# Writing out the feed-forward loops of a two-layer decoder kernel, and giving each modulation slab its own tabled place

## The chip, the cores and the metric

One core of one Trainium2 chip runs the whole program: TensorE (PE), VectorE (DVE), ScalarE (ACT), GpSimd (POOL) and SyncE (SP), each with its own instruction stream, tied together by semaphores. The metric is device time of one execution in microseconds; lower is better. Before the change it was 2439.5 us (median of 3 runs, 2437.03 to 2441.91).

## The reference

Two layers of a decoder, 256 tokens, width D = 2048, all in float32:

```python
for l in range(2):
    mod = silu(c) @ w_mod[l] + b_mod[l]                 # 12288 values
    sh1, sc1, g1, sh2, sc2, g2 = split(mod, 6)
    u = x * (1 + sc1) + sh1
    proj = u @ w_in[l]                                  # 2048 x 6144: q k v B C h
    attn = dilated_mixture(rotary(q), rotary(k), v)     # 8 heads
    conv = B * conv3(C * h)
    mixed = group_rms_norm([attn, conv]) * gain
    x = layer_norm(alpha * x + (1 + g1) * (mixed @ w_out[l]))
    u = x * (1 + sc2) + sh2
    ff = relu(u @ w_ff1[l]) ** 2 @ w_ff2[l]             # hidden width 8192
    x = layer_norm(alpha * x + (1 + g2) * ff)
```

## The kernel before

**Units and groups.** The large products are cut into units. A unit is 512 output columns over a contraction of 2048, for both 128-token tiles. It has eight groups (j = 0 to 7) of 256 contraction rows, and a group is 12 matmuls of 128x128 by 128x512: each float32 weight is split into a high and a low part, each activation too, and hi·hi, lo·hi and hi·lo are summed (L1150 to L1152). A layer is a mixer of 16 units (12 of `w_in`, 4 of `w_out`) and a feed-forward part of 32 units: four blocks of 4 units up (`w_ff1`) and 4 down (`w_ff2`). Below, a place "p" in a part is 8 · unit + j, and a side job at p comes behind group p.

**The path of a weight.** SP loads a group's weights (512 KB) into one of four `raw` buffers as soon as `lo_ready` says that DVE has read it. ACT copies it to `w_hi` (L388) once PE has finished the group four back; DVE subtracts and writes `w_lo` (L677); PE multiplies.

**Modulation.** `w_mod` is 24 slabs of 1024 columns by 2048 rows, each 16 chunks of 512 KB. POOL loads chunks into four `mod_raw` buffers as they come free. DVE multiplies each chunk by the condition and adds it to one of two accumulators `mod_acc` (L688 for the first of a slab, L692 for the rest). When a slab's 16 chunks are in, it has to be summed over the partitions by PE before its accumulator is used again: `reduce_slab` does it with 8 matmuls with one column (L1175), and DVE adds the bias into `mod_col`. A gate is wanted along the free axis, on all partitions: `gate_slab` (L1195) does that with two 128x512 matmuls, and DVE adds the result to `gate`, into which the bias has been loaded by a broadcast DMA. Slabs 0 to 3 are made in the start, 4 to 9 in the first mixer, 10 to 17 in the first feed-forward part and 18 to 23 in the second mixer; the second feed-forward part has no chunks. Each layer has 12 slabs; its first gate is slabs 4 and 5 (16 and 17 in the second layer), its last gate slabs 10 and 11 (22 and 23).

**What sets the order.** Each engine's order is written by hand. In the mixers it is written out, with side jobs at tabled places (`MIX_MOD_AT` for chunks, `RED_AT` for sums). In the feed-forward part PE, ACT and DVE run a loop of three turns over 8 units (`Fori`, L1380, L624, L1036), and the last 7 units are written out behind it. In the first layer's loop there are four chunks per unit, and PE sums a slab behind (v, j) = (4, 1) and (7, 7), where the second one's last chunk is at (7, 6). The last gate of the first layer is summed into `mod_col` like the others, and then brought to the free axis by `gate_rows`: 16 matmuls (L1186) and four copies on ACT. The gates of slabs 16, 17 and 22, 23 are left in `mod_acc` until the next fill unit.

**Fill units.** Between two parts x is normalised: DVE's residual and statistics, ACT's normalisation, PE's transposes (L1203), ACT's and DVE's split. The unit that follows is a fill unit (fills 1, 2 and 3 stand between the four parts). In fills 2 and 3 PE sums both gate slabs behind j = 5. In fill 1 the sum of slab 9 comes first: PE does it at the mixer's end and DVE reads it within `statistics`.

**Hidden activations.** After an up unit ACT makes relu and square into `hid`, PE transposes it (behind j = 2 of the next unit), and ACT and DVE split it into `m_hi` and `m_lo`. All transposes and sums share two PSUM banks `tb` in a fixed numbering of jobs.

Of the kernel before, what the change touches and what calls it, by code (L numbers as in the profile page):

```python
# [30 lines left out]
ALU = mybir.AluOpType  # L31
# [38 lines left out]
LOOP_H = (0, 2, 4, 6)  # L70
MOD_LAYER = MIX_SLABS + 8
# [16 lines left out]
def taken(layer):  # L88

    return set(Q_AT[layer] + K_AT[layer] + O_AT[layer] + Z_AT + B_AT + R_AT  # L90
               + [start + 3 for g in range(2) for start in HEAD_AT[layer][g]])
# [3 lines left out]
RED_AT = [[min(p for p in range(MIX_MOD_AT[layer][KC * (i + 1) - 1] + 2, 8 * U_MIX) if p not in taken(layer))  # L95
           for i in range(MIX_SLABS - 1)] for layer in range(DEPTH)]


def gate_half(layer, i):

    first = 0 if layer == 0 else 4
    return i - first if i - first in (0, 1) else None
# [13 lines left out]
def transpose_jobs():  # L116
# [8 lines left out]
    for layer in range(DEPTH):  # L125
        modded = layer < DEPTH - 1
        if layer == 0:
            for q in range(START_SLABS):
                add(("start turn", 2 * q), 1)
                add(("start", q), 1)  # L130
                add(("start turn", 2 * q + 1), 1)
        else:
            add(("fill", 2 * layer), 8)
            add(("rows", 2 * layer), 4)
        side = []
        for g in range(2):
# [5 lines left out]
        side += [(p, -1, 0, "red", 2 if layer == 0 and i < 2 else 1, i) for i, p in enumerate(RED_AT[layer])  # L142
                 if not (layer and gate_half(layer, i) is not None)]
        for _, _, _, name, count, i in sorted(side):
            add((name, layer, i), count)
        if modded:
            add(("red", layer, 5), 1)
        add(("fill", 2 * layer + 1), 8)
        if not modded:
            add(("rows", 2 * layer + 1), 4)  # L150
        add(("loop", layer), 3 * (8 + 2 * modded))
        add(("last h0", layer), 2)
        if modded:
            add(("last gate", layer), 4)
        add(("last h1", layer), 6)
# [3 lines left out]
def build(nc, x, cond_c, ln_cols, w_in, w_out, w_ff1, w_ff2, w_mod, b_mod, b_rows, conv_w, mix_g, ln1_g, ln1_b,  # L159
# [3 lines left out]
    with ctx:  # L163
# [130 lines left out]

        def at(b, per, const):

            return const if b is None else b * per + const
# [76 lines left out]
        def _(act):  # L374
# [71 lines left out]
            def fill_unit(fill, unit, side):  # L446
# [3 lines left out]
                if fill >= 2:  # L450
                    load_gate_bias(fill - 1)
# [22 lines left out]
            def relu_square(b, u0):  # L474

                par = u0 % 2
                act.wait_ge(pair_used, at(b, 64, 8 * u0 + 8))
# [3 lines left out]
                act.wait_ge(acc_read[par], at(b, 4, u0 // 2 + 1))  # L481
                nc.scalar.activation(hid[:], hid[:], ACT.Square).then_inc(hid_ready, 1)
# [111 lines left out]
            def gate_rows(job0):  # L594

                for i in range(4):
                    job = job0 + i
                    wait_job(act, job)
                    nc.scalar.activation(gate[:, i * NCOL:(i + 1) * NCOL], tb[job % 2][:],
                                         ACT.Identity, bias=1.0).then_inc(t_read[job % 2], 1)  # L600

            def hidden(layer, b, s, block_no, job0):

                per = 8 + 2 * (layer < DEPTH - 1)
                for i in range(2):
                    n = at(b, 8, SPLITS * layer + 24 + 8 * block_no + 2 * s + i)
                    bank = (job0 + i) % 2
                    split(n, i, at(b, per, job0 + i), bank, m_hi, 4 * s + 2 * i)
                    split_high(at(b, per // 2, (job0 + i) // 2 + 1), i, bank, m_hi, 4 * s + 2 * i)

            def mlp(layer):
                base = U_LAYER * layer + U_MIX

                def after_up(j):
                    if j == 7:
                        relu_square(None, base)
# [7 lines left out]
                with act.Fori(0, BLOCKS - 1) as b:  # L624
                    for v in range(8):
                        for j in range(GROUPS):
                            ahead(b * 8 + (base + 1 + v), j)
                            if v < 4 and j == 2:
                                hidden(layer, b, v, 0, JOB[("loop", layer)] + LOOP_H[v])
                        if v in (0, 1, 2, 7):  # L630
                            relu_square(b, base + 1 + v)
                last = base + 8 * (BLOCKS - 1) + 1
                final = layer == DEPTH - 1
                for v in range(7):
                    for j in range(GROUPS):
                        if not (final and v == 6 and j + AHEAD >= GROUPS):
                            ahead(last + v, j)
                        if v < 4 and j == 2:
                            job0 = JOB[("last h0", layer)] if v == 0 else JOB[("last h1", layer)] + 2 * (v - 1)
                            hidden(layer, None, v, BLOCKS - 1, job0)  # L640
                        if not final and v == 0 and j == 5:
                            gate_rows(JOB[("last gate", layer)])
                        if v == 4 and j == 0:
# [3 lines left out]
                    if v < 3:  # L647
                        relu_square(None, last + v)
# [17 lines left out]
        def _(dve):  # L666
# [29 lines left out]
            def mod_next(q, loop=None):  # L696

                k, par = q % KC, q // KC % 2
                first = START_SLABS * KC
                if loop is None:  # L700
                    count = (first + q, 16 * (q // MODS + 1))
                else:
                    count = (loop * 32 + (first + q), loop * (16 * 32 // MODS) + 16 * (q // MODS + 1))
                mod_step(None, k, par, mod_raw[:, q % MODS, :], mod_in[q % MODS], count)

            def reduced(n, job, bank, loop_n=None):

                wait_job(dve, job)
                if loop_n is None:
                    cols = slice(n * SC, (n + 1) * SC)  # L710
                    o, b = mod_col[:, cols], mod_b[:, cols]
                else:
                    o, b = mod_col[:, bass.ds(loop_n, SC)], mod_b[:, bass.ds(loop_n, SC)]
                nc.vector.tensor_tensor(o, tb[bank][:, 0:SC], b, ALU.add).then_inc(t_read[bank], 1)
# [34 lines left out]
            def statistics(fill, slab=None):  # L749
# [5 lines left out]
                if slab is not None:  # L755
                    reduced(slab[0], slab[1], slab[1] % 2)
                    dve.wait_ge(t_read[slab[1] % 2], slab[1] // 2 + 1)
# [38 lines left out]
            def fill_unit(fill, unit, side, slab=None):  # L796
                statistics(fill, slab)
# [6 lines left out]
                for j in range(GROUPS):  # L804
# [4 lines left out]
                    if fill >= 2 and j == 5:  # L809
                        gate_sum(0, JOB[("rows", fill)], fill)  # L810
                        gate_sum(1, JOB[("rows", fill)] + 2, fill)
# [10 lines left out]
            def start_scale(q):  # L822

                job = JOB[("start", q)]
                reduced(q, job, job % 2)
# [657 lines left out]
```

## Time and profile before

| | us |
|---|---|
| median of 3 runs | 2439.5 (2437.03 to 2441.91) |
| the profiled execution | 2438.73 |
| its span, first to last instruction | 2437.0 |
| PE busy | 2284.5 (94%) |
| DVE busy | 1725.1 (71%) |
| ACT busy | 1108.1 (45%) |
| w_lo (L677), 768 of 1225 ns | 938.2 |
| chunks (L692) from mod_raw, 300 of 1280 ns | 383.9 |
| DMA | 622.20 MB, 255 GB/s |

Matmuls are pipelined: a 128x512 matmul is shown with 0.39 us, but in a full stretch the next one starts 0.227 us later, so a group takes 2.72 us and a unit 21.76. What is read below is therefore the time from one start to the next. The granted clock is shown as 1.0 for 2.4 GHz and 0.5 for 1.2 GHz. Starts are in us from the span's start. The first mixer ends at about 497 us, the first feed-forward part at 1259, the second mixer at 1676 and the second feed-forward part at 2415.

### The profile page before, as it was taken

Reading aid. Unit: us, or ns where it says so; the run is one execution under the profiler, and the core shown is the slowest. Engines: PE = TensorE matmul, PEld = TensorE weight load, DVE = VectorE, ACT = ScalarE, POOL = GpSimd, SP = SyncE. Lnnn points to the kernel's source line nnn. Section 1 sums busy time; section 2 is a strip of 40 time slices with the busy share of each in tenths; the row PEclk is TensorE's granted clock in tenths of the full one; section 3 lists DMA queues with packets and bytes.
Section 4 is the critical chain, followed back from the end, with each engine's and each line's share of the span. In section 5 each row is a group of like instructions: output and inputs, shape, how many; then the busy total and the mean of one; then the engine's idle time right before and its main releaser. Section 6 shows DMA issues by size and latency. Waiting matters only on the chain.

```text
span 2437.0 us, 31367 instructions
## 1 busy us (share of the span) xinstructions
PE 2284.5 (94%) x10440; PEld 1893.1 (78%) x10440; DVE 1725.1 (71%) x1897; ACT 1108.1 (45%) x1378; POOL 203.0 (8%) x388
## 2 busy tenths in 40 slices
PE   3689999989999999999989999997999999999996
PEld 2577887868878878888867888876788888888885
DVE  6889888977756666676889878888655445455566
ACT  2235643365435435445444554434553553543542
POOL 2211111101000000010100111110000000000000
PEclk9789999999999999999989999999999999999998
DMA  9987888948878887887976888897566666666663
GB/s 355 376 292 285 312 319 316 342 158 293 273 260 264 277 288 240 279 290 232 340 258 210 286 294 297 316 318 247 163 188 193 189 186 195 183 189 191 189 219 110
DMA packets 174528, 622.20 MB, mean 255 GB/s; under 512 B 19648, under 2 KB 20416, under 8 KB 174016
## 3 DMA queue, kind: packets, MB, share of 16 engines
q1 hardware_dynamic: 114064, 407.50, 49.6%
q0 software_dynamic: 55296, 201.35, 24.2%
q10 hardware_dynamic: 5040, 11.54, 1.5%
q8 instruction: 93, 1.52, 0.3%
q14 instruction: 35, 0.29, 0.0%
HBM read 618.22 MB, written 2.10 MB: 255 GB/s over the span
## 4 chain that ended last, share of the span: by engine, by line
PE 79%; DVE 11%; issue 4%; DMA 3%; ACT 2%; ACTq 1%; SPq 0%; DVEq 0%; POOLq 0%
PE bank L1150 25%; PE bank L1152 24%; PE bank L1151 24%; DVE mod_acc L692 5%; PE bank L1203 2%; DVE w_lo L677 2%; PE bank L1175 2%; ACT w_hi L388 1%; DMA raw<-w_out_dram 1%; ACT utmp L405 1%; DMA mod_raw<-w_mod_dram 1%; DMA raw<-w_ff_dram 1%; DVE xt L857 1%; ACTq L427 1%; DMA Z<-w_mod_dram 1%
## 5 line engine op out<-in xcount | busy, mean ns | idle before, releaser
L677 DVE TENSOR_TENSOR w_lo<-raw,w_hi 128x1024 fp32r<-128x1024 f32 x768 | 938.2, 1225 | 620.0 <-ACT w_hi L388 617.9
L388 ACT ACTIVATE w_hi<-raw 128x1024 fp32r<-128x1024 f32 x768 | 812.4, 1060 | 1165.9 <-PE bank L1152 1018.8
L1150 PE MATMUL bank<-w_hi,u_hi 128*128 128x512 f32 x1792 | 719.6, 402 | 10.5 <-issue 8.4
L1151 PE MATMUL bank<-w_hi,u_lo 128*128 128x512 f32 x1792 | 705.1, 393 | 0.0
L1152 PE MATMUL bank<-w_lo,u_hi 128*128 128x512 f32 x1792 | 705.0, 393 | 0.0
L1150 PE MATMUL bank<-w_hi,m_hi 128*128 128x512 f32 x1280 | 502.2, 392 | 5.6 <-DVE m_lo L728 4.0
L1152 PE MATMUL bank<-w_lo,m_hi 128*128 128x512 f32 x1280 | 500.1, 391 | 0.0
L1151 PE MATMUL bank<-w_hi,m_lo 128*128 128x512 f32 x1280 | 499.8, 390 | 0.0
L1150 PEld LDWEIGHTS bank<-w_hi,u_hi 128*128 128x128 f32 x1792 | 341.4, 191 | 81.1 <-issue 10.0
L1152 PEld LDWEIGHTS bank<-w_lo,u_hi 128*128 128x128 f32 x1792 | 340.7, 190 | 73.0
L1151 PEld LDWEIGHTS bank<-w_hi,u_lo 128*128 128x128 f32 x1792 | 341.6, 191 | 69.3 <-issue 1.0
L692 DVE SCALAR_TENSOR_TENSOR mod_acc<-mod_raw,cond,mod_acc 128x1024 f32<-128x1024 f32 x300 | 383.9, 1280 | 1.4 <-DMA mod_raw<-w_mod_dram 1.2
L1150 PEld LDWEIGHTS bank<-w_hi,m_hi 128*128 128x128 f32 x1280 | 241.3, 188 | 56.9 <-DVE m_lo L728 4.8
L371 POOL DMA_DIRECT2D mod_raw<-w_mod_dram x316 | 166.9, 528 | 1374.6 <-DVE mod_acc L692 1139.4
L1152 PEld LDWEIGHTS bank<-w_lo,m_hi 128*128 128x128 f32 x1280 | 241.1, 188 | 50.4
L1151 PEld LDWEIGHTS bank<-w_hi,m_lo 128*128 128x128 f32 x1280 | 241.3, 189 | 49.4
L1175 PE MATMUL bank<-ones,mod_acc 128*128 128x1 f32 x288 | 40.5, 271 | 50.7 <-DVE mod_acc L692 50.3
L1175 PEld LDWEIGHTS bank<-ones,mod_acc 128*128 128x128 f32 x288 | 40.7, 223 | 54.5 <-DVE mod_acc L692 27.2
L692 DVE SCALAR_TENSOR_TENSOR mod_acc<-Z,cond,mod_acc 128x1024 f32<-128x1024 f32 x60 | 77.0, 1283 | 7.4 <-DMA Z<-w_mod_dram 3.7
L1203 PE MATMUL bank<-idn,xt 128*128 128x128 f32 x128 | 25.1, 347 | 55.0 <-ACT xt L439 28.9
L1203 PEld LDWEIGHTS bank<-idn,xt 128*128 128x128 f32 x128 | 19.1, 177 | 59.7 <-ACT xt L439 29.8
L728 DVE TENSOR_TENSOR m_lo<-utmp,m_hi 128x512 fp32r<-128x512 f32 x72 | 49.3, 692 | 12.8 <-ACT m_hi L412 12.8
(110 smaller groups left out, 938.9 us busy)
## 6 DMA issues: line engine op xcount, KB each, us to landing
raw<-w_ff_dram SPq DMA_DIRECT2D x512, 512.0 KB, 4.2
mod_raw<-w_mod_dram POOLq DMA_DIRECT2D x320, 512.0 KB, 6.1
raw<-w_in_dram SPq DMA_DIRECT2D x192, 512.0 KB, 5.6
Z<-w_mod_dram POOLq DMA_DIRECT2D x64, 512.0 KB, 8.9
raw<-w_out_dram SPq DMA_DIRECT2D x64, 512.0 KB, 7.0
Z<-ln_g_dram ACTq DMA_DIRECT2D x16, 256.0 KB, 7.0
Z<-ln_b_dram ACTq DMA_DIRECT2D x16, 256.0 KB, 8.8
gate<-b_rows_dram ACTq DMA_DIRECT2D x3, 1024.0 KB, 4.7
```

Of the source, the lines that this page charges most:

```text
L371: pool.dma_start(mod_raw[:, k:k + 1, :], chunk(r * MODS + (first + k))).then_inc(mod_in[k], 16)
L388: nc.scalar.activation(w_hi[:, j % AHEAD, :], raw[:, j % RAW, :], ACT.Copy).then_inc(hi_ready, 1)
L405: ins = nc.scalar.activation(utmp[:, slot, c * SEQ:(c + 1) * SEQ], tb[bank][:, c * SEQ:(c + 1) * SEQ], ACT.Identity, bias=bias, scale=scale)
L427: act.dma_start(lngb[:, s, a, :], src[layer:layer + 1, s * NCOL:(s + 1) * NCOL] .to_broadcast([P, NCOL])).then_inc(gb_in[s], 16)
L677: nc.vector.tensor_tensor(w_lo[:, j % AHEAD, :], raw[:, j % RAW, :], w_hi[:, j % AHEAD, :].bitcast(F32), ALU.subtract).then_inc(lo_ready, 1)
L692: ins = nc.vector.scalar_tensor_tensor(out=a, in0=src, scalar=cond[:, k:k + 1], in1=a, op0=ALU.mult, op1=ALU.add)
L728: nc.vector.tensor_tensor(lo[:, chunk:chunk + 2, :], src, hi[:, chunk:chunk + 2, :].bitcast(F32), ALU.subtract).then_inc(split_ready, 1)
L1150: nc.tensor.matmul(o, hi[:, k, tok], wh, start=(k == 0), stop=False)
L1151: nc.tensor.matmul(o, lo[:, k, tok], wh, start=False, stop=False)
L1152: ins = nc.tensor.matmul(o, hi[:, k, tok], wl, start=False, stop=(k == KC - 1))
L1175: ins = nc.tensor.matmul(b[:, c:c + 1], mod_acc[:, par, c * P:(c + 1) * P], ones[:, 0:1], start=True, stop=True)
L1203: ins = nc.tensor.transpose(b[:, c * SEQ + t * P:c * SEQ + (t + 1) * P], src(c, t), idn[:])
```

## The change

1. The feed-forward loops of PE, ACT and DVE are gone; all 31 units behind the fill unit are written out. SP's and POOL's loops stay.
2. One table `MOD_AT` says for each chunk of slabs 4 to 23 at which place DVE adds it, and `RED_AT` derives from it where the slab is summed: two places behind its last chunk, or at the next free place. Slabs 16 and 17 are held back to places 8 and 12 of the second mixer.
3. Slabs per part are now 6, 8, 4 and 2: the last gate of the second layer (slabs 22, 23; 32 chunks) moves from the second mixer to the second feed-forward part, at one or two chunks per unit in its units 1 to 24.
4. All gate slabs are summed with `gate_slab` and `gate_sum`; `gate_rows` is gone, and `load_gate_bias` is called in fill 1 too.
5. Slab 9 is summed at place 124 of the first mixer, not at its end.

```diff
-MIX_SLABS = 6
-MIX_MOD_AT = [([17] * 4 + [p for p in range(18, 8 * 16) if p % 8 != 7])[:MIX_SLABS * KC],
-              [8 * u + j for u in range(1, 16) for j in range(7) if j != 3 or u >= 9][:MIX_SLABS * KC]]
-FF_MOD_AT = (1, 3, 4, 6)
+MIX_SLABS = (6, 4)
+FF_SLABS = (8, 2)
+    mixer0 = ([17] * 4 + [p for p in range(18, 8 * U_MIX) if p % 8 != 7])[:MIX_SLABS[0] * KC]
+    ff0 = sorted([8 * w + j for w in range(1, FF_UNITS - 1) for j in (1, 3, 4, 6)]
+                 + [8 * w + 7 for w in (1, 2, 3, 9, 10, 11, 17, 18)])
+    mixer1 = sorted([8 * u + j for u in range(1, 15) for j in (0, 2, 4, 6) if u + j > 1]
+                    + [8 * u + 1 for u in (1, 2, 3, 4, 9, 10, 11, 12, 13)])
+    ff1 = sorted([8 * w + 4 for w in range(1, 25)] + [8 * w + 1 for w in range(1, 9)])
...
+RED_NOT_BEFORE = {16: MIXER_AT[1] + 8, 17: MIXER_AT[1] + 12}
+def red_positions():
+    out = {}
+    for i in range(SLABS - START_SLABS):
+        n = START_SLABS + i
+        p = max(MOD_AT[KC * (i + 1) - 1] + 2, RED_NOT_BEFORE.get(n, 0))
+        while p in TAKEN or p in out:
+            p += 1
+        out[p] = n
+    return out
...
 PE:
-                with pe.Fori(0, BLOCKS - 1) as b:
-                    for v in range(8):
...
-                            if modded and (v, j) in ((4, 1), (7, 7)):
...
-                        if modded and v == 0 and j == 5:
-                            gate_rows(6 * layer + 5, JOB[("last gate", layer)], loop0 + 9)
+                for w in range(1, FF_UNITS):
+                    block_no, s = divmod(w, 8)
+                    up = s < 4
+                    unit_groups(base + w, u_hi if up else m_hi, u_lo if up else m_lo,
+                                operand=SPLITS * layer + 24 + 8 * block_no if s == 4 else None,
+                                side=lambda j: side(w, j))
...
-                    if fill >= 2 and j == 5:
-                        gate_slab(0, JOB[("rows", fill)], steps)
-                        gate_slab(1, JOB[("rows", fill)] + 2, steps)
...
-                if layer < DEPTH - 1:
-                    reduce_slab(1, JOB[("red", layer, 5)],
-                                steps=(START_SLABS + layer * MOD_LAYER + 6) * KC)
+            def slab_sum(p):
+                n = RED_AT.get(p)
+                if n in GATE_SLABS:
+                    gate_slab(n % 2, JOB[("red", n)], (n + 1) * KC)
+                elif n is not None:
+                    reduce_slab(n % 2, JOB[("red", n)], (n + 1) * KC)
 ACT:
-                if fill >= 2:
-                    load_gate_bias(fill - 1)
+                load_gate_bias(fill)
```

DVE and ACT get the same loop over `w` in place of their `Fori`; the semaphore counts that were sums of a register and a number are numbers now.

The tables give these places for the sums: first mixer 33, 52, 69, 87, 106 (as before) and 124; first feed-forward part 35, 67, 94, 125, 153, 184; second mixer 8, 12, 36, 67, 92, 120 (before: 30, 52, 73, 91); second feed-forward part 70 and 198.

PE at the end of the loop's body in the first feed-forward part, before (L1150 to L1152 are a group's matmuls, L1175 the sum of a slab, L1380 the loop):

```order
L1150 MATMUL bank<-w_hi,u_hi 128x512
L1151 MATMUL bank<-w_hi,u_lo 128x512
L1152 MATMUL bank<-w_lo,u_hi 128x512
L1173 REGISTER_ALU
L1175 MATMUL bank<-ones,mod_acc 128x1 x8
L1380 REGISTER_ALU
L1380 COMPARE_AND_BRANCH
L1150 MATMUL bank<-w_hi,u_hi 128x512
L1151 MATMUL bank<-w_hi,u_lo 128x512
L1152 MATMUL bank<-w_lo,u_hi 128x512
```

and PE around slab 11 (half of a gate, L1152 here), which the loop's first turn summed at that border and which is now summed behind group 3 of the next unit (L1119 to L1121 are the three matmuls):

```order
L1119 MATMUL bank<-w_hi,u_hi 128x512
L1120 MATMUL bank<-w_hi,u_lo 128x512
L1121 MATMUL bank<-w_lo,u_hi 128x512
L1152 MATMUL bank<-mod_acc,ones 128x512 x2
L1119 MATMUL bank<-w_hi,u_hi 128x512
L1120 MATMUL bank<-w_hi,u_lo 128x512
L1121 MATMUL bank<-w_lo,u_hi 128x512
```

The register instructions and the branch are gone, and the sum stands between two groups of one unit.

DVE at the end of the second mixer's last unit, up to the statistics, before (L692 adds a chunk, L677 writes `w_lo`, L854 to L862 are `residual`):

```order
L692 SCALAR_TENSOR_TENSOR mod_acc<-mod_raw,cond,mod_acc 128x1024
L677 TENSOR_TENSOR w_lo<-raw,w_hi 128x1024
L692 SCALAR_TENSOR_TENSOR mod_acc<-mod_raw,cond,mod_acc 128x1024
L677 TENSOR_TENSOR w_lo<-raw,w_hi 128x1024 x2
L854 TENSOR_TENSOR bank<-bank,gate 128x512 x2
L857 SCALAR_TENSOR_TENSOR xt<-xt,bank 128x512 x2
L862 BN_STATS stats<-xt 128x6 x2
L752 BN_AGGR mv<-stats 128x2 x2
```

and after (L681 writes `w_lo`, L859 to L867 are `residual`, L724 reads a slab's sum):

```order
L867 BN_STATS stats<-xt 128x6 x2
L681 TENSOR_TENSOR w_lo<-raw,w_hi 128x1024
L724 TENSOR_TENSOR mod_col<-bank,mod_b 128x8
L681 TENSOR_TENSOR w_lo<-raw,w_hi 128x1024 x7
L859 TENSOR_TENSOR bank<-bank,gate 128x512 x2
L862 SCALAR_TENSOR_TENSOR xt<-xt,bank 128x512 x2
L867 BN_STATS stats<-xt 128x6 x2
L763 BN_AGGR mv<-stats 128x2 x2
```

The unit's six chunks (the last two stand above) are gone from between the `w_lo` instructions; the sum of slab 21 is read behind the first of them.

## Rows read from the trace of the kernel before

**Rows 1.** Page: chain by engine; costliest PE group (count | busy, mean ns | idle before).

```profile
PE 79%; DVE 11%; issue 4%; DMA 3%; ACT 2%; ACTq 1%; SPq 0%; DVEq 0%; POOLq 0%
...
L1150 PE MATMUL bank<-w_hi,u_hi 128*128 128x512 f32 x1792 | 719.6, 402 | 10.5 <-issue 8.4
```

**Rows 2.** Two stretches; columns: us, busy PE, PEld, DVE, ACT, POOL, clock, DMA share, GB/s.

```profile
1609.00:1676.00 67.00, 65.42 (x287) 53.38 (x285) 60.04 (x60) 23.96 (x23) 8.97 (x17) 1.00 0.93 334
1724.00:2415.00 691.00, 689.68 (x3105) 571.84 (x3103) 358.63 (x340) 329.61 (x359) 0.00 (x0) 1.00 0.62 187
```

**Rows 3.** Source L1380, the loop's branch on PE; ns, min/median/max.

```profile
L1380 PEldq COMPARE_BRANCH  x6: 83/4386/5272, 717.8 to 2254.7; - x6
```

**Rows 4.** Waits of PE, 700 to 1100 us; total, times, longest.

```profile
PE bank L1175 <- DVE mod_acc L692: 2.7, 3, 0.9
```

**Rows 5.** PE timeline, a slab sum amid a unit, then the loop's ends.

```profile
633.17 1.84 PE L1175 MATMUL bank<-ones,mod_acc 128*128 128x1 f32 x16
...
717.67 1.95 PE L1175 MATMUL bank<-ones,mod_acc 128*128 128x1 f32 x16 [0.89 <-DVE mod_acc L692]
723.39 0.79 PE L1150 MATMUL bank<-w_hi,u_hi 128*128 128x512 f32 x1 [3.77 <-issue]
...
728.67 0.48 PE L1150 MATMUL bank<-w_hi,u_hi 128*128 128x512 f32 x1
...
912.10 0.79 PE L1150 MATMUL bank<-w_hi,u_hi 128*128 128x512 f32 x1 [3.50 <-issue]
...
917.02 0.39 PE L1150 MATMUL bank<-w_hi,u_hi 128*128 128x512 f32 x1
...
1096.71 0.49 PE L1150 MATMUL bank<-w_hi,u_hi 128*128 128x512 f32 x1
...
1101.14 0.40 PE L1150 MATMUL bank<-w_hi,u_hi 128*128 128x512 f32 x1
```

**Rows 6.** PE timeline, `gate_rows`.

```profile
1115.68 3.90 PE L1186 MATMUL bank<-idn,mod_col 128*128 128x128 f32 x32
```

**Rows 7.** PE timeline, the gate slabs of fill 2 and of fill 3.

```profile
1291.88 2.26 PE L1195 MATMUL bank<-mod_acc,ones 128*128 128x512 f32 x4
1296.48 1.98 PE L1195 MATMUL bank<-mod_acc,ones 128*128 128x512 f32 x4 [2.35 <-DVE gate L723]
1297.90 0.80 PE L1150 MATMUL bank<-w_hi,u_hi 128*128 128x512 f32 x1
...
1710.34 2.26 PE L1195 MATMUL bank<-mod_acc,ones 128*128 128x512 f32 x4
...
1717.42 1.41 PE L1150 MATMUL bank<-w_hi,u_hi 128*128 128x512 f32 x1
```

**Rows 8.** PE timeline, second mixer from 1508 us, then fill 3 and fill 2.

```profile
1508.60 1.95 PE L1175 MATMUL bank<-ones,mod_acc 128*128 128x1 f32 x16 [0.37 <-DVE Z L922]
1510.41 0.70 PE L1150 MATMUL bank<-w_hi,u_hi 128*128 128x512 f32 x1
...
1514.14 0.39 PE L1150 MATMUL bank<-w_hi,u_hi 128*128 128x512 f32 x1
...
1642.77 0.50 PE L1150 MATMUL bank<-w_hi,m_hi 128*128 128x512 f32 x1 [1.41 <-DVE w_lo L677]
...
1687.85 1.97 PE L1203 MATMUL bank<-idn,xt 128*128 128x128 f32 x8 [11.68 <-ACT xt L439]
...
1267.88 1.97 PE L1203 MATMUL bank<-idn,xt 128*128 128x128 f32 x8 [9.14 <-ACT xt L439]
```

**Rows 9.** Waits of all engines, 1609 to 1676 us.

```profile
ACT w_hi L388 <- DMA raw<-w_out_dram: 29.8, 16, 4.4
```

**Rows 10.** PE timeline, end of the first mixer and fill 1.

```profile
436.54 1.92 PE L1175 MATMUL bank<-ones,mod_acc 128*128 128x1 f32 x16 [0.71 <-DVE mod_acc L692]
...
497.13 1.84 PE L1175 MATMUL bank<-ones,mod_acc 128*128 128x1 f32 x16
507.04 1.97 PE L1203 MATMUL bank<-idn,xt 128*128 128x128 f32 x8 [8.06 <-ACT xt L439]
```

More of the change, by code:

```diff
@@ L85 @@
 R_AT = [76, 100]
[L88 to L102, printed above, removed]
+TAKEN = set()
+for _layer in range(DEPTH):
+    TAKEN |= {MIXER_AT[_layer] + _p
+              for _p in (Q_AT[_layer] + K_AT[_layer] + O_AT[_layer] + Z_AT + B_AT + R_AT
+                         + [_start + 3 for _g in range(2) for _start in HEAD_AT[_layer][_g]])}
+    TAKEN |= {FF_AT[_layer] + 8 * _w + HID_J for _w in range(FF_UNITS) if 1 <= _w % 8 <= 4}
+GATE_SLABS = {12 * layer + 6 * part + 4 + half: (2 * layer + part, half)
+              for layer in range(DEPTH) for part in range(2) for half in range(2)}
+RED_NOT_BEFORE = {16: MIXER_AT[1] + 8, 17: MIXER_AT[1] + 12}
[7 more added lines that the diff above has]
+        out[p] = n
+    return out
+RED_AT = red_positions()
 START_UNITS = 3
@@ L141, in transpose_jobs @@
                      (R_AT[g], g, 6, "r", 2, g)]
[L142 to L143 removed]
+        first, last = MIXER_AT[layer], FF_AT[layer]
+        side += [(p - first, -1, 0, "red", 2 if n in GATE_SLABS else 1, n) for p, n in RED_AT.items()
+                 if first <= p < last]
         for _, _, _, name, count, i in sorted(side):
[L145 to L147 removed]
+            add((name, i) if name == "red" else (name, layer, i), count)
         add(("fill", 2 * layer + 1), 8)
[L149 to L155, printed above, removed]
+        side = [(8 * (8 * block + s + 1) + HID_J, "hid", 2, (block, s)) for block in range(BLOCKS) for s in range(4)]
+        side += [(p - last, "red", 2 if n in GATE_SLABS else 1, n) for p, n in RED_AT.items()
+                 if last <= p < last + 8 * FF_UNITS]
+        for _, name, count, i in sorted(side):
+            add((name, i) if name == "red" else (name, layer) + i, count)
     return at
@@ L592, in mixer, with turned @@
                                 start_fill(q + 1)
[L594 to L604, printed above, removed]
+            def turned(layer, block_no, s):
                 for i in range(2):
[L606 to L609, printed above, removed]
+                    job = JOB[("hid", layer, block_no, s)] + i
+                    n = SPLITS * layer + 24 + 8 * block_no + 2 * s + i
+                    split(n, i, job, job % 2, m_hi, 4 * s + 2 * i)
+                    split_high(job // 2 + 1, i, job % 2, m_hi, 4 * s + 2 * i)
             def mlp(layer):
@@ L1167, in unit_groups, with reduce_slab @@
                         side(j)
-            def reduce_slab(par, job, bank=None, reads=None, steps=None):
-                b = begin_job(job, bank, reads)
+            def reduce_slab(par, job, steps):
+                b = begin_job(job)
                 pe.wait_ge(mod_used, steps)
```

279 lines of the change are left out of this document (99 added, 180 removed).

## The prediction

> **What bounds the kernel now.** I read the page first: of the chain that ended last, 79% is PE and 11% DVE [rows 1]. Then I went through PE's timeline unit by unit, since every part has the same groups, and asked where two matmuls start more than 0.227 us apart. In the second feed-forward part almost nowhere: PE is busy 689.68 of 691 us at full clock, with DVE at 358.63 and DMA at 0.62 [rows 2]. The time that can be won lies in a few places: the ends of the loop, the two fill units that sum gates, the second mixer's last third, and the waits of the fill units. All terms below are PE time at such places, as PE sets the end nearly everywhere.
>
> **The loop's ends in the first feed-forward part.** The loop's body has its second slab sum last. Its chunk is added only one group earlier, so PE waits for DVE: 2.7 us in three turns, 0.89 each [rows 4]. Then PE stands idle, for 3.77 us behind the first turn and 3.50 behind the second, waiting for nothing that the profile shows [rows 5]. The branch explains it: PE's six records of it last 83 ns when it falls through and up to 5272 ns when it is taken (median 4386) [rows 3]. It is issued as soon as the sum is, and PE was not ahead, because its sequencer had just been held by the wait. After it the granted clock is at 1.2 GHz: the 12 matmuls from 723.39 take until 728.67, 5.28 us where 2.72 are normal, those from 912.10 take 4.92, those from 1096.71 take 4.43 [rows 5]. So the three turns lose 0.89 + 3.77 + 2.56 = 7.2, 0.89 + 3.50 + 2.20 = 6.6 and 0.89 + 1.71 = 2.6: 16.4 us. Written out, there is no branch, and each sum stands two groups behind its last chunk. That is enough: with one group between, PE came 0.89 us early, and one group more is 2.72. The sum itself stays at 1.84 us [rows 5], as at 633.17, where PE did not wait. Gain 16.4.
>
> The Trainium skill, "Advanced Engine Details and Errata", section on control flow timing, gives about 108 ns for a compare-and-branch; this trace disagrees for a taken one on PE, with 5.27 us, and agrees only for the one that falls through (0.083). By the page's figure the idle time would have another cause and could stay; that is weighed as a rival below.
>
> **The loop's ends in the second.** There is no sum at the loop's end, PE's sequencer is ahead, and little of the branch is left to see: of 8.4 us that L1150 waited on "issue" in the whole span [rows 1], 3.77 and 3.50 are the two above, and 1.1 us is all that remains. Gain 1.1.
>
> **`gate_rows`.** 16 matmuls, 3.90 us on PE in one piece [rows 6], gone. What takes their place, `gate_slab` for slabs 10 and 11 in place of `reduce_slab`, costs about the same as these: in fill 2 two gate slabs last from 1291.88 to 1297.90, 6.02 us, of which 2.35 is a wait, so 1.84 each [rows 7]. ACT's four copies go too, and cost nothing now. DVE gets gate sums of about 1.3 us each, in units where it has room. Gain 3.9.
>
> **The gates in the fill units.** Fill 2: four jobs share two banks, so the third waits 2.35 us for DVE [rows 7]. Moved to places 8 and 12 of the second mixer there are two jobs at a time and no such wait: gain 2.35. DVE turns q at place 7 and reads the sum behind it, and PE's next job in these banks is at place 10; I count at most 0.5 us of wait there. Fill 3: 7.08 us from 1710.34 to 1717.42, and the first matmul behind is shown with 1.41 us where it was 0.80 in fill 2, as the clock had fallen. The two sums still cost 3.7, in the second feed-forward part. Gain 7.08 - 3.7 + 0.6 = 4.0. The 32 chunks that go there cost nothing: 32 x 1.28 = 41 us more on DVE, which is idle for 332 of 691 us, and 16.8 MB over some 520 us, 32 GB/s more where DMA is at 187 GB/s and a share of 0.62, against 334 to 0.93 in the mixer [rows 2].
>
> **The second mixer.** In its last third each unit now has 7 chunks. DVE is busy 60 of 67 us and DMA at 0.93 [rows 2], and ACT waits 29.8 us for `w_out` [rows 9]. This reaches PE as 1.41 us at 1642.77, and in fill 3: PE is idle 11.68 us where it was idle 9.14 in fill 2, which has a lighter unit before it [rows 8]. After the change these units have 5, 5, 4 and no chunks, a load like that before fill 2 or less. Gain 1.4 + 2.5. The slab sum at place 73 follows the transposes at 72 and waits 0.37 us for their bank; the clock then falls, and the nine steps from 1510.41 to 1514.14 take 3.73 us where 2.04 are normal [rows 8]. At place 67 there is no such neighbour. Gain 0.4 + 1.7 = 2.1. Together 6.0, with ends at 0 (DMA stays the bound) and 8.5 (the other small waits of this part go too).
>
> **What it costs: slab 9.** Its sum is now hidden, more or less: PE does it at 497.13, and fill 1 takes 9.91 us from there to the first transpose, of which 8.06 is idle [rows 10]. Fill 2, without a sum, has 9.14 idle [rows 8]: 0.77 shorter in all by the rows, of which I count 0.6. At place 124 the sum is on the path: 1.84 us. The last chunk is at 122, but in this stretch DVE lags (7 chunks a unit), and the same distance at place 106 gave a wait of 0.71 [rows 10], so I add 0.8; and behind such waits the clock fell each time (at 723, 1096 and 1510), some 1.5 us. Loss 1.84 + 0.8 + 1.5 - 0.6 = 3.5, with ends at 1.0 (no wait, clock kept) and 4.5.
>
> **Moved or added without a price.** `load_gate_bias` in fill 1 is one more DMA of 1 MB on ACT's queue, issued while `raw` is full and ACT works, as in fills 2 and 3. The first feed-forward part has eight chunks more in its first 18 units (five in a unit instead of four); DVE then has 8 x 1.225 + 5 x 1.28 + 1.4 = 17.6 us of work in a unit of 22.7.
>
> **Sum.** 16.4 + 1.1 + 3.9 + 2.35 + 4.0 + 6.0 - 3.5 = 30.3 us off the profiled execution's own 2438.73 (span 2437.0 and 1.7 around it): 2408.4. The median of the runs lies 0.8 above it: 2409 us. With the ends of the mixer's and slab 9's terms and 1 us for the small ones, 2403 to 2419.
>
> **The rivals.**
> - The written-out code is fetched late (slower). PE's feed-forward stream is now 62 units long instead of 8 that repeat; if the sequencer runs dry at some borders, each costs what a taken branch costs, 3.8 to 5.3 us. It decides from 7 such stalls on (30.3 / 4.4); one in every four units makes 15 x 4.4 = 66, so 2475 us. Against it: both mixers, 32 units with the same density, are written out already, and all of the 8.4 us on "issue" [rows 1] is at the loops' ends; and a mixer's fetches compete with a DMA share of 0.93 [rows 2]. 3 in 100. The Trainium skill, "Runtime: NRT & Kernel Launch", section on instruction fetch mechanics, says that an engine fetches 16 KiB blocks ahead by itself and that the cost at a block's border is mostly hidden: by it this case costs nothing, and the mixers' rows agree.
> - The loop's idle time is not the branch (a restart of PE behind the wait): then the 8.4 us on "issue" and the low clock behind the first two, 2.56 + 2.20, stay, 13 us: 2422. Against it: the wait is only 0.89, and at 1096 the same wait and sum, with a branch not taken, has no idle time behind. 4 in 100.
> - The second mixer stays as slow as it is, since its bound is the weights' DMA, and slab 9 costs its full 4.5: 2409 + 6 + 1 = 2416. For it: 29.8 us of waits for `w_out`. Against: these DMAs queue beside 512 KB chunks that now go. 13 in 100.
> - Each new sum place finds its own wait with a fall of the clock behind, 0.9 + 1.7 for most of the eight moved sums: 18 us back, 2427. Against it: two groups of distance and light units. 6 in 100.
> - The change moves nothing in PE's path: only if another engine bounded these places, which the timeline excludes. 2 in 100.
>
> **How the numbers follow.** The forecast has 72 in 100 and 2409 us. The range reaches from 2400 (all small gains come) to 2423, which takes in the DMA case and the restart case. What a measurement of this kernel can tell from no change is 0.2%, 4.9 us. Slower: the first rival and a remainder, 4 in 100; the same: 3; faster: 93.
>
> **What would show it.** PE has no COMPARE_BRANCH record and no idle time "issue" behind 500 us; the sums at places 35, 67 and so on stand at 1.84 with no wait; L1186 is gone; fills 2 and 3 have no L1195, and fill 3's idle time is near 9.1; the second feed-forward part has two L1195 pieces and stays at 2.72 us a group; at place 124 of the first mixer PE waits for L1175's chunk. The prediction is wrong if PE's groups in the written-out parts take more than 2.72 us without a side job, if PE stands idle for "issue" where the loop's ends were, or if fill 3's idle time stays above 11 us.

## The result, and the profile of the changed kernel

The changed kernel takes 2410.57 us (median of 4 runs, 2409.49 to 2412.88). The kernel before, run beside it on the same chip, took 2440.70 (4 runs, 2437.03 to 2442.04). The ratio is 0.9887 [0.9875, 0.9899]: faster by 1.1%. The forecast was 2409 with a range of 2400 to 2423. The profiled execution's span is 2407.8 us, against 2437.0.

The page of the changed kernel, its chain by engine, its costliest PE group and the DMA queue that brings instructions:

```profile
PE 85%; DVE 9%; issue 3%; ACT 2%; DMA 1%; ACTq 0%; SPq 0%; DVEq 0%; POOLq 0%
...
L1119 PE MATMUL bank<-w_hi,u_hi 128*128 128x512 f32 x1792 | 717.5, 400 | 5.7 <-DVE u_lo L739 5.7
...
q8 instruction: 82, 1.34, 0.2%
```

The 8.4 us on "issue" of [rows 1] are gone from the group. It now waits for DVE's `u_lo` alone. PE's share of the chain rose from 79% to 85% (83% in the second profile of this kernel). The last row (packets, MB, share) had 93 packets before: written-out code is fetched with fewer packets than the loops.

PE's waits over the whole span (total, times, longest), without those for `xt` and `utmp` and four for `Z` and `gate` of 1.1 and less:

```profile
PE bank L1143 <- DVE mod_acc L696: 46.9, 5, 21.9
...
PE bank L1119 <- DVE u_lo L739: 5.7, 4, 1.8
PE bank L1119 <- DVE m_lo L739: 3.3, 2, 2.0
PE bank L1119 <- DVE w_lo L681: 1.2, 1, 1.2
```

The slab sums (L1143) waited 50.3 us in 8 places before and wait 46.9 in 5 now. Four of the five stand in the start, one at place 106 of the first mixer (0.71). Of the four waits for `u_lo`, three last 1.80, one in each fill unit. That row matters below.

Two stretches, the last 67 us of the second mixer (it ends at 1651 us here) and most of the second feed-forward part, to be laid beside [rows 2] (us, busy PE, PEld, DVE, ACT, POOL, clock, DMA share, GB/s):

```profile
1584.00:1651.00 67.00, 65.80 (x299) 54.33 (x297) 50.83 (x52) 24.18 (x23) 5.28 (x10) 1.00 0.86 295
1700.00:2385.00 685.00, 685.00 (x3081) 567.07 (x3080) 394.50 (x370) 322.66 (x353) 14.79 (x28) 1.00 0.65 209
```

In the mixer the DMA share fell from 0.93 to 0.86 and DVE's busy time from 60.04 to 50.83 us. The second feed-forward part took on 32 chunks, and PE is busy for all of its 685 us.

PE's timeline of the changed kernel at the places of [rows 7, 8, 10] (slab 11's sum at 707.89 is the one of [rows 5]'s first loop end):

```profile
487.66 1.92 PE L1143 MATMUL bank<-ones,mod_acc 128*128 128x1 f32 x16
507.02 1.97 PE L1168 MATMUL bank<-idn,xt 128*128 128x128 f32 x8 [9.13 <-ACT xt L464]
...
707.89 1.88 PE L1152 MATMUL bank<-mod_acc,ones 128*128 128x512 f32 x4
...
1274.88 0.50 PE L1119 MATMUL bank<-w_hi,u_hi 128*128 128x512 f32 x1 [1.80 <-DVE u_lo L739]
1283.20 1.88 PE L1152 MATMUL bank<-mod_acc,ones 128*128 128x512 f32 x4
...
1616.51 0.50 PE L1119 MATMUL bank<-w_hi,m_hi 128*128 128x512 f32 x1 [1.20 <-DVE w_lo L681]
...
1660.43 1.97 PE L1168 MATMUL bank<-idn,xt 128*128 128x128 f32 x8 [9.14 <-ACT xt L464]
...
1687.27 0.50 PE L1119 MATMUL bank<-w_hi,u_hi 128*128 128x512 f32 x1 [1.80 <-DVE u_lo L739]
```

Place 124's sum (487.66) did not wait. Slab 11's sum (707.89) does not wait, and fill 3's idle time fell from 11.68 to 9.14. In fills 2 and 3 the gate sums are gone, and a wait of 1.80 for `u_lo` stands where there was none in [rows 7].

**Where the time went.** I number the 96 units from 0 and measure each from its first matmul's start to that of the next unit. Units 16, 48 and 64 are the fill units; the idle time before a fill's transposes falls into units 15, 47 and 63. The differences before minus after, in us:

| stretch | units | forecast | measured |
|---|---|---|---|
| start | up to 3 | 0 | 1.4 |
| slab 9 at place 124, fill 1 | 15, 16 | -3.5 | -3.7 |
| first loop ends and `gate_rows` | 17 to 46 | 20.3 | 21.6 |
| gates out of fill 2 | 48, 49 | 2.35 | 0.4 |
| second mixer | 50 to 63 | 6.0 | 7.4 |
| gates out of fill 3, their sums later | 64, 72, 88 | 4.0 | 0.6 |
| second loop ends | 73, 80, 81 | 1.1 | 1.6 |
| sum | | 30.3 | 29.3 |

So the total was right with two terms too large by 5.4 together, and the rest too small by 4.4. The table lays one profiled execution beside one other. The experiments ask which of these are the change and which the single execution.

### The profile page after: what moved, and what is told of

Read it like the earlier page. It is cut to its first block, busy times and chain, and to the rows that moved or that the text cites. A ratio compares the mean times of both kernels' runs of the same rounds, so it can differ in the third digit from the quotient of the medians.

```text
span 2407.8 us, 30138 instructions
## 1 busy us (share of the span) xinstructions
PE 2271.3 (94%) x10384; PEld 1882.3 (78%) x10384; DVE 1727.3 (72%) x1899; ACT 1105.3 (46%) x1374; POOL 203.1 (8%) x388
## 4 chain that ended last, share of the span: by engine, by line
PE 85%; DVE 9%; issue 3%; ACT 2%; DMA 1%; ACTq 0%; SPq 0%; DVEq 0%; POOLq 0%
PE bank L1119 27%; PE bank L1121 27%; PE bank L1120 26%; DVE mod_acc L696 4%; PE bank L1168 2%; PE bank L1143 1%; DVE w_lo L681 1%; ACT w_hi L413 1%; ACT utmp L430 1%; DVE xt L798 1%; PE bank L1152 0%; DMA Z<-w_mod_dram 0%; DVE xt L801 0%; DMA lnc<-ln_cols_dram 0%; DMA raw<-w_out_dram 0%
## 5 line engine op out<-in xcount | busy, mean ns | idle before, releaser
L681 DVE TENSOR_TENSOR w_lo<-raw,w_hi 128x1024 fp32r<-128x1024 f32 x768 | 937.7, 1224 | 595.2 <-ACT w_hi L413 593.0
L1119 PE MATMUL bank<-w_hi,u_hi 128*128 128x512 f32 x1792 | 717.5, 400 | 5.7 <-DVE u_lo L739 5.7
L1121 PE MATMUL bank<-w_lo,u_hi 128*128 128x512 f32 x1792 | 702.9, 392 | 0.0
L1119 PE MATMUL bank<-w_hi,m_hi 128*128 128x512 f32 x1280 | 501.1, 391 | 4.5 <-DVE m_lo L739 3.3
L1121 PE MATMUL bank<-w_lo,m_hi 128*128 128x512 f32 x1280 | 498.9, 390 | 0.0
L1119 PEld LDWEIGHTS bank<-w_hi,u_hi 128*128 128x128 f32 x1792 | 340.2, 190 | 76.6 <-DVE u_lo L739 7.3
L1121 PEld LDWEIGHTS bank<-w_lo,u_hi 128*128 128x128 f32 x1792 | 339.2, 189 | 72.6
L1119 PEld LDWEIGHTS bank<-w_hi,m_hi 128*128 128x128 f32 x1280 | 240.8, 188 | 55.3 <-DVE m_lo L739 4.2
L1121 PEld LDWEIGHTS bank<-w_lo,m_hi 128*128 128x128 f32 x1280 | 240.7, 188 | 50.4
L1143 PE MATMUL bank<-ones,mod_acc 128*128 128x1 f32 x256 | 36.4, 272 | 46.9 <-DVE mod_acc L696 46.9
L1143 PEld LDWEIGHTS bank<-ones,mod_acc 128*128 128x128 f32 x256 | 37.1, 226 | 49.5 <-issue 26.4
```

The source lines that it names most:

```text
L681: nc.vector.tensor_tensor(w_lo[:, j % AHEAD, :], raw[:, j % RAW, :], w_hi[:, j % AHEAD, :].bitcast(F32), ALU.subtract).then_inc(lo_ready, 1)
L1119: nc.tensor.matmul(o, hi[:, k, tok], wh, start=(k == 0), stop=False)
L1121: ins = nc.tensor.matmul(o, hi[:, k, tok], wl, start=False, stop=(k == KC - 1))
L1143: ins = nc.tensor.matmul(b[:, c:c + 1], mod_acc[:, par, c * P:(c + 1) * P], ones[:, 0:1], start=True, stop=True)
```

## The experiments

**The changed kernel once more**, unaltered.

> The changed kernel once more, unaltered, to see what a place's time is worth. The first unit behind fill 1 took 27.73 us here against 25.80 before the change, though nothing in it was changed but the matmul clock (the granted clock came back later). Theory A: the clock comes back at a moment that has nothing to do with the program, so the three first units behind the fills (27.73, 27.35, 27.85 us) move by up to 2 us each in another execution, and the rest stays within 0.1 us. Rival B: they are set by the program and repeat within 0.1 us.

Measured: 2415.06 us (one run), span 2413.4, kernel before alongside 2438.98 (11 runs). Units 16, 48 and 64 took 27.55, 27.20 and 27.66 where they had taken 27.73, 27.35 and 27.85. Unit 15 took 41.51 where it had taken 37.64. PE's row of place 124's sum:

```profile
491.75 1.92 PE L1143 MATMUL bank<-ones,mod_acc 128*128 128x1 f32 x16 [2.23 <-DVE mod_acc L696]
```

The fill units of the changed kernel therefore repeat to 0.2, close to the rival's 0.1. What varies most is the end of the first mixer, where DVE is late by an amount that differs between executions: in the five profiles with this place (this kernel twice, and three of its variants below) the sum waited 0, 0.42, 0.62, 2.23 and 2.23. Units 12 and 13 moved too, from 30.02 and 26.15 to 32.51 and 24.49. The start, up to unit 3, takes 189.7 to 192.5 in all ten profiles, so its 1.4 in the table is not the change.

**Only PE's feed-forward loop written out**, in the kernel before; the sums stay at the loop's end.

```diff
-                with pe.Fori(0, BLOCKS - 1) as b:
+                for b in range(BLOCKS - 1):
```

> The kernel before with PE's two feed-forward loops alone written out; ACT and DVE keep theirs, chunks and sums stay where they were. Theory (the taken branch is PE's idle time): the 3.77, 3.50 and 1.1 us of idle time without a releaser go; the three waits of 0.89 us for the last chunk stay, and a fall of the clock behind each of them costs 1.7, as behind the third turn. Gain 8.4 + 2.56 + 2.20 - 3.4 = 9.8 us, so about 2431. Rival (a restart of PE behind the wait): nothing goes, 2440. Rival (written-out code is fetched late): new idle time without a releaser appears, and it is slower than 2440.

Measured: 2426.52 us (2423.39 to 2432.71), ratio 0.9952 [0.9937, 0.9967]. PE at the first turn's end, the sum and the next turn's first matmul:

```profile
720.97 1.92 PE L1175 MATMUL bank<-ones,mod_acc 128*128 128x1 f32 x16 [0.98 <-DVE mod_acc L692]
722.75 0.48 PE L1150 MATMUL bank<-w_hi,u_hi 128*128 128x512 f32 x1
```

The wait for DVE stays (0.98, was 0.89), and the 3.77 of idle time behind it is gone: the two have different causes, and the idle time is the branch. By units, the loop's ends gave 3.85 + 2.53 + 3.49 + 0.57 + 0.08 = 10.5 in the first part and 1.7 in the second. That is 12.2 where I expected 9.8, mainly because the clock stayed up behind the first of the three waits. The restart rival, by which the idle time stays, is excluded.

**Only the last chunk earlier**, in the kernel before; the loop and its branch stay.

```diff
-FF_MOD_AT = (1, 3, 4, 6)
+FF_MOD_AT = (0, 1, 3, 4)
```

> The kernel before with the chunks of the first feed-forward part at j = 0, 1, 3, 4 of a unit in place of 1, 3, 4, 6, so that the loop's second sum stands three groups behind its last chunk; the loop stays. Theory A (the branch is hidden when PE's sequencer is ahead, as in the second layer's loop, and the wait is what exposes it): the waits of 0.89 go and the idle time behind the taken branches falls from 3.77 and 3.50 to at most 1.5 each; gain 2.7 + 4.5 to 7.3 + 3 of clock, so 2427 to 2430. Rival B (a taken branch stands idle for its 5 us whatever goes before): only the waits go, gain 2.7 to 4.4, so 2436 to 2438.

Measured: 2428.91 us (2428.18 to 2435.23), ratio 0.9965 [0.9951, 0.998]. The same place, and the branch's records over the span:

```profile
718.50 1.84 PE L1175 MATMUL bank<-ones,mod_acc 128*128 128x1 f32 x16
722.68 0.49 PE L1150 MATMUL bank<-w_hi,u_hi 128*128 128x512 f32 x1 [2.34 <-issue]
...
L1380 PEldq COMPARE_BRANCH  x6: 83/3625/4232, 718.2 to 2244.5; - x6
```

The wait is gone and the idle time is not: 2.34 of a branch of 4.23 us that began at 718.16, and 1.87 behind the second turn, each with a fall of the clock behind (units 25 and 33 are 1.7 and 2.1 longer than in the changed kernel). The time lies in the first theory's stretch, but the idle times are above its 1.5, so the result stands between the two: without the wait a part of the branch is hidden, but not all. In five of the eight taken branches of this kernel and of the one before, exactly 17 matmuls start while the branch lasts, and 14 or 15 in the others; in all but one the next matmul starts 0.28 us after its end. I read from this that about 17 matmuls stand queued when PE's sequencer is ahead. At 0.227 each they cover 3.9 us, which is why the second part, without a sum at this place, lost so little: its branches of 3.79 and 4.99 us left 0 and 1.15 us of idle time. When 16 of them are the one-column ones of a sum (1.84 us for all), they cover half of that.

**The last gate back in the second mixer**: the changed kernel with slabs 22 and 23 added there, as before, and summed in the first units of the second feed-forward part.

```diff
-MIX_SLABS = (6, 4)
-FF_SLABS = (8, 2)
+MIX_SLABS = (6, 6)
+FF_SLABS = (8, 0)
...
-RED_NOT_BEFORE = {16: MIXER_AT[1] + 8, 17: MIXER_AT[1] + 12}
+RED_NOT_BEFORE = {16: MIXER_AT[1] + 8, 17: MIXER_AT[1] + 12, 22: FF_AT[1] + 12, 23: FF_AT[1] + 20}
```

The mixer's chunks go to the places that they had in the kernel before.

> The changed kernel with the last gate's 32 chunks back in the second mixer (96 chunks there, at the places of before but one later at the start), their two sums at places 12 and 20 of the second feed-forward part. Everything else as changed. Theory: the second mixer loses what it won beyond the sums: the wait of 1.4 us for w_lo, 2.5 us of idle time in fill 3 and part of the 2.1 at the middle; 5 to 8 us slower than the changed kernel, so 2416 to 2419. Rival (the mixer's gain came from the places of the sums, not from the chunks): within 2 us of the changed kernel, 2411 to 2413.

Measured: 2418.34 us (2415.15 to 2421.14), ratio 0.9917 [0.9898, 0.9936], where the changed kernel has 0.9887. The two intervals touch, so the units say more: 50 to 63 together took 5.0 us more than in the changed kernel. The row of fill 3:

```profile
1666.72 1.97 PE L1167 MATMUL bank<-idn,xt 128*128 128x128 f32 x8 [11.86 <-ACT xt L463]
```

Its idle time is back at 11.86, where [rows 8] has 11.68. In this pair of profiles the move of the chunks earned the 2.7 of fill 3, and 2.3 at other places. The part of the theory on `w_lo` failed: with the chunks back its waits here are 0.9 in sum, where the changed kernel has 1.20 and 1.47 in its two profiles. And the 2.7 is an upper value: the two kernels above, written-out loop and earlier chunk, have the chunks in the mixer too, and fill 3 is idle for 10.36 and 10.91 in them.

**The sums of slabs 9 and 21 back at the mixers' ends**, in the changed kernel.

```diff
-RED_NOT_BEFORE = {16: MIXER_AT[1] + 8, 17: MIXER_AT[1] + 12}
+RED_NOT_BEFORE = {16: MIXER_AT[1] + 8, 17: MIXER_AT[1] + 12, 9: MIXER_AT[0] + 127, 21: MIXER_AT[1] + 127}
```

> The changed kernel with slab 9 summed behind the last group of the first mixer again (place 127, not 124) and slab 21 behind the last group of the second mixer (127, not 120), where PE waits for the fill unit anyway. Theory A (a sum ahead of the end costs its full 1.84 us, one at the end is hidden in the fill unit's idle time): 1.8 + 1.8 us, idle time in fills 1 and 3 falls from 9.13 to about 7.3, so 3.6 us faster than the changed kernel, about 2407. Rival B (DVE reads the sum late and its residual, the head of the fill's chain, starts later): the idle time falls by less than 1.84 each, and the gain is under 2 us.

Measured: 2408.95 us (2407.92 to 2410.31), ratio 0.9876 [0.9858, 0.9895]. Fills 1 and 3:

```profile
507.43 1.97 PE L1168 MATMUL bank<-idn,xt 128*128 128x128 f32 x8 [8.79 <-ACT xt L464]
...
1660.03 1.97 PE L1168 MATMUL bank<-idn,xt 128*128 128x128 f32 x8 [7.53 <-ACT xt L464]
```

In fill 3 the sum lies in the idle time, which shrinks from 9.14 to 7.53, and unit 63 is 1.77 us shorter: a sum at place 120 costs its full 1.84, at 127 almost nothing. In fill 1 only 0.68 came, with the clock's part behind (unit 16) at -0.55. There the comparison is weak, since unit 15 takes 37.64 to 41.51 in the five profiles with place 124, and 37.64 is the shortest. Both intervals overlap, so the two median times show nothing by themselves; the fills' rows do.

**The last fill job one group earlier**: in the changed kernel, ACT's and DVE's second half of a fill's split.

```diff
-                    if j in (1, 4):
+                    if j in (1, 3):
```

(in both engines' fill units).

> The changed kernel with ACT's and DVE's last two fill jobs behind j = 3 of the fill unit, not j = 4. It asks where the gain of moving the gates out of fills 2 and 3 went: a wait of 1.80 us for u_lo at j = 6 stands in all three fills after the change and stood only in fill 1 before. Theory A (the gates' wait of 2.35 us had covered it; ACT does these jobs only once PE has finished group 4): the 1.80 us go in all three, 5.4 us, about 2405. Rival B (the transposes or DVE's gain steps bound it): the wait stays above 1 us, or moves to another group; 2409 to 2412.

Measured: 2407.47 us (2406.04 to 2409.91), ratio 0.9871 [0.9852, 0.989]. The median is 3.1 below the changed kernel's, with intervals that overlap; the units decide. Units 16, 48 and 64 fell from 27.73, 27.35 and 27.85 to 25.75, 24.66 and 25.79: the wait of 1.80 is gone in all three. DVE's timeline of the changed kernel shows what had been late in fill 2:

```profile
1271.80 1.29 DVE L801 TENSOR_TENSOR xt<-xt,Z 128x512 f32<-128x512 f32 x2
1273.01 1.22 DVE L681 TENSOR_TENSOR w_lo<-raw,w_hi 128x1024 fp32r<-128x1024 f32 x1
1274.15 1.28 DVE L739 TENSOR_TENSOR u_lo<-utmp,u_hi 128x512 fp32r<-128x512 f32 x2
```

PE has come to the group that needs `u_lo` at 1273.09, and DVE has the gain and shift of `xt` and a `w_lo` in front of it. One new wait came in the next unit, at 1290.68, where the changed kernel has none:

```profile
1290.68 1.16 PE L1168 MATMUL bank<-idn,Z 128*128 128x128 f32 x8 [1.58 <-DVE gate L734]
```

It takes back 1.81: the transposes at place 10 need a bank that slab 16's gate sum holds until DVE has read it.

**PE kept busy in the fills**: the changed kernel with 36 matmuls, whose result nobody reads, ahead of the transposes of each fill.

```diff
+                pe.wait_ge(s_read, 8 * ((fill + 1) // 2))
+                for _ in range(36):
+                    nc.tensor.matmul(sbank[:], m_hi[:, 0, 0:P], m_hi[:, 0:2, :], start=True, stop=True)
```

> The changed kernel with 36 added 128x512 matmuls (8.2 us) at the head of each fill unit on PE, whose results nobody reads, so that PE is busy in the three idle stretches of 9.13 us. Theory A (behind a fill's idle time the clock is at 1.2 GHz for 13.7 us, which costs about 2 us in the first unit and 1 us in the transposes on the chain): gain 2 to 3 us a fill, 6 to 9 in all, about 2403. Rival B (the clock falls anyway, or the added matmuls end late and hold up the chain): 2409 to 2414.

Measured: 2415.00 us (2411.02 to 2417.19), ratio 0.9903 [0.9884, 0.9922]: no faster. The stretch of fill 3 in the changed kernel, and then, here, place 124's sum, fills 1 and 2, the same stretch of fill 3 and the place of fill 2's `u_lo` wait:

```profile
1655.00:1670.00 15.00, 8.83 (x29) 7.01 (x30) 8.90 (x23) 8.71 (x16) 0.00 (x0) 0.54 0.28 102
```

```profile
491.51 2.15 PE L1143 MATMUL bank<-ones,mod_acc 128*128 128x1 f32 x16 [2.23 <-DVE mod_acc L696]
512.46 1.09 PE L1168 MATMUL bank<-idn,xt 128*128 128x128 f32 x8 [0.99 <-ACT xt L464]
...
1252.93 1.09 PE L1168 MATMUL bank<-idn,xt 128*128 128x128 f32 x8 [0.99 <-ACT xt L464]
...
1659.00:1674.00 15.00, 12.39 (x62) 9.86 (x61) 9.65 (x25) 10.09 (x18) 0.00 (x0) 1.00 0.32 108
...
1276.00:1286.00 10.00, 9.09 (x33) 7.35 (x34) 8.55 (x13) 3.71 (x5) 0.00 (x0) 0.83 0.43 120
```

The changed kernel's granted clock over fill 3 is 0.54, mostly 1.2 GHz; here it is 1.00. The transposes last 1.09 instead of 1.97. Units 47, 63 and 64 gained 0.8, 0.8 and 2.06, and unit 48 nothing: in fills 1 and 2 the clock fell again behind the wait for `u_lo` (0.83 in the last row). Unit 15 lost 3.06 by the wait of 2.23 at place 124, which the unaltered kernel shows too, and the fall of the clock behind it. So I overrated it: fill 2 gained 0.7 and fill 3 gained 2.9, and the whole fits neither of my two stretches.

**All of it**: the changed kernel with the three edits above, 28 such matmuls in fills 1 and 3 and 36 in fill 2, and slab 8's sum at place 108 instead of 106.

```diff
+RED_NOT_BEFORE = {16: MIXER_AT[1] + 8, 17: MIXER_AT[1] + 12, 8: MIXER_AT[0] + 108,
+                  9: MIXER_AT[0] + 127, 21: MIXER_AT[1] + 127}
...
+                for _ in range(36 if fill == 2 else 28):
```

> The changed kernel with the three edits above together (28 added matmuls in fills 1 and 3, where the sum takes the first 1.84 us of the idle time, 36 in fill 2), and slab 8 summed at place 108 of the first mixer, not 106, where PE waits 0.71 us for its last chunk and the clock then falls. Theory: 3.6 + 7 + 5.4 + 2 = 18 us below the changed kernel, 2392. Rival (the edits share the same idle time, so that part of each is counted twice): 2396 to 2402.

Measured: 2397.83 us (2397.03 to 2399.41, 5 runs), ratio 0.9832 [0.9817, 0.9848], against 2438.71 of the kernel before alongside. It is faster than both kernels. Slab 8's sum, the first transposes of fills 1, 2 and 3, and the stretch of fill 3:

```profile
440.44 1.84 PE L1144 MATMUL bank<-ones,mod_acc 128*128 128x1 f32 x16
...
506.52 1.54 PE L1169 MATMUL bank<-idn,xt 128*128 128x128 f32 x8 [4.11 <-ACT xt L465]
...
1245.13 1.09 PE L1169 MATMUL bank<-idn,xt 128*128 128x128 f32 x8 [0.98 <-ACT xt L465]
...
1652.92 1.09 PE L1169 MATMUL bank<-idn,xt 128*128 128x128 f32 x8 [1.02 <-ACT xt L465]
...
1645.00:1660.00 15.00, 12.36 (x63) 9.85 (x63) 10.67 (x26) 8.02 (x15) 0.00 (x0) 1.00 0.42 137
```

Against the changed kernel unit 13 gained 2.55 (slab 8's sum now stands four groups behind its last chunk instead of two: no wait of 0.71 and no fall of the clock), but unit 12 lost 0.89; 16 gained 2.53, 48 gained 3.67, 63 gained 2.58, 64 gained 4.18, 15 lost 0.73, and 49 lost 1.81 by the same wait of 1.58. The clock stays up through fill units 2 and 3. In units 16 and 48 the edits together gave about 1 us more each than the sum of what they gave alone; in unit 64 they gave 0.6 less. So they help each other in part.

The time lies in the rival's stretch, 6 us above the 2392 that I expected. Two places account for most of it: fill 1, where units 15 and 16 gave 1.8 together and PE still stands idle for 4.11 us with transposes of 1.54, and the loss in unit 49. No run has these edits without the added matmuls, so what they give in this company is not shown separately.

## Why the prediction was right, and where it was wrong

**The loop's ends and `gate_rows`: right.** 21.6 measured for 20.3, 1.6 for 1.1. In the first part the two edits done alone give 10.5 and 9.2 of it: the branch alone leaves the waits of 0.98 and a fallen clock behind two of three (0.83 over 10 us), the distance alone leaves 2.34 and 1.87 of the branch and the fallen clock behind both. Step "PE was not ahead, because its sequencer had just been held by the wait" is true only in part. It was also not ahead because the matmuls queued there were a sum's, short ones. In the forecast both edits came together, so the error cost nothing.

On this branch the Trainium skill, "Runtime: NRT & Kernel Launch", section on instruction fetch mechanics, says that a taken branch to a target outside the fetched pages stalls until these are fetched. The traces agree: 3.49 to 5.27 us for each taken one, 0.083 for those not taken, and no such idle time in the written-out code. They show the fetch itself too. In each of the eight taken branches one 16 KB packet of the instruction queue starts 1.1 to 2.8 us after the branch does, and the branch ends 1.4 to 1.6 us after it has landed; no packet falls into the four that were not taken. The queue in the first taken branch's own time, 717.8 to 723.1 us, before:

```profile
q8 instruction: 1, 0.02, 1.1%
```

**Fills 2 and 3: wrong, the steps "gain 2.35" and "gain 4.0".** Measured 0.4 and 0.6. In this pair of profiles each fill unit did get 3.99 shorter (units 48 and 64), but with 7.1 (two sums, in fill 3) or 6.0 (fill 2) taken out. I priced what goes and did not ask what is late next: `u_lo` was due in the same group, hidden behind the gate sums' time. Fill 1, a fill unit without gate sums, showed it in the kernel before:

```profile
531.48 0.50 PE L1150 MATMUL bank<-w_hi,u_hi 128*128 128x512 f32 x1 [1.80 <-DVE u_lo L728]
```

I had read fill 1's idle time and not its waits. The last-fill-job run shows it by taking the wait away.

How much is missing is less sure than that something is. The two variants of the kernel before have the same fill units as it has, and these took 31.81 and 33.67 (fill 2) and 33.82 and 31.46 (fill 3) where it took 31.34 and 31.84. Against the mean of the three, with the moved sums counted, the gains are 1.4 in fill 2 and 1.1 in fill 3: still short of 2.35 and 4.0, but more than the table has.

**The second mixer: 7.4 for 6.0 in this pair of profiles, wrong in its parts.** Fill 3's 2.5 came, as 2.7. That 2.7 is one execution against another: against the idle times of the written-out and earlier-chunk kernels it is 1.2 and 1.8. The 1.4 at 1642 stayed, as 1.20 at 1616.51. The 1.7 for the clock behind place 73's sum should not have been counted as the change's: both kernels with the old tables of the mixer (loop written out; chunk earlier) have the same wait there,

```profile
1501.08 1.95 PE L1175 MATMUL bank<-ones,mod_acc 128*128 128x1 f32 x16 [0.36 <-DVE Z L922]
```

and the clock stays at 1.00 around it (here a stretch of the written-out one; it is 0.91 over the same stretch of the profile that I read):

```profile
1500.00:1520.00 20.00, 19.64 (x111) 16.80 (x110) 15.03 (x24) 7.60 (x9) 2.65 (x5) 1.00 0.89 314
```

Their units 57 and 60 are 1.6 us shorter each than in the profile that I read. In unit 60 it is the same again: behind a wait of 1.95 for `m_lo` that all three have, the clock is 0.67 over 1601 to 1606 in the profile that I read, and 1.00 over the same place of both others. So some 3.2 of the 7.4 were one execution's clock. The change's own part is not fixed better than between 2 and 5: units 50 to 63 take 358.3 and 358.7 in the changed kernel, 360.2 with the loop written out, 361.5 with the chunk earlier and 363.2 with the last gate back. The term of 6.0 was too large.

**Slab 9: right in size (-3.7 for -3.5), by other parts.** The wait of 0.8 did not come in this execution (in the kernel's second profile it was 2.23), and 1.9 came in unit 16, which took 27.73 for 25.81. But the two kernels that keep the old place took 27.23 and 27.88 there, so this part is not shown to be the change's. That the term fits to 0.2 is luck. Over all profiles with the old and the new place, units 15 and 16 together take 61.7, 66.1 and 64.9 before, and 65.4, 69.1 and 66.2 after (without the runs that changed fill 1 too): a mean of 64.2 against 66.9, so 2.7, from three profiles each that spread over 4 us.

**The sum.** By its own ends the stretch of the sum reaches 2417 (2409 + 6 + 1 + 1), not 2419; nothing hangs on it. With the means above in place of single profiles, and the start at nothing, the stretches add up to 25 to 28 us, not 29.3. So the mechanism of the largest term is right, but that the total came within 2 us of the forecast is partly luck: fill and mixer terms that were too large stand against falls of the clock and a start that happened to favour this pair of profiles. The medians are 30.1 apart in this result, and 28.4 if the 11 runs of the kernel before beside the first experiments stand in for its 4.

**The rivals.** No fetch stall appeared (instruction packets fell from 93 to 82). The sums at their new places do not wait in the first feed-forward part. In the second mixer transposes waited, once the fill unit was quicker, for a bank that a sum held. DMA did not keep the second mixer as slow as it was, but ACT still waits 21.0 us for `w_out` over its last 67 us, where it waited 29.8 [rows 9].

## What to carry to other kernels

Before you count a stall as gained, look for the same place without it: a sibling stage shows what is late next. When a loop on PE has one short instruction group ahead of its branch, put long matmuls there (the second layer's loop, which has them, lost 0 and 1.15 us) or write the loop out. Read a fall of the clock behind a short wait in more than one execution before you put a price on its removal.

## What the runs showed of the hardware that I had not expected

- A taken branch on PE lasts 3.5 to 5.3 us, with one 16 KB instruction packet in it, but what is seen of it depends on what stands in the queue: about 17 matmuls, so 3.9 us of 128x512 ones or 1.9 us of a sum's.
- Behind the same wait of 0.36 to 0.37 us before a sum the granted clock fell in one execution and not in two others, at a cost of 1.6 us.
- DVE's lateness at the first mixer's end varies between executions of the same program by 2.2 us, about as much as the term of fill 2's gates.
- Matmuls that nobody reads keep the clock at 2.4 GHz (1.00) through 9 us of waiting, and the transposes behind run in 1.09 instead of 1.97 us. Alone they made the kernel no faster; behind the wait of 1.80 that was left in fills 1 and 2 the clock fell all the same.
